# A re-ordered front end in a two-block transformer kernel: index logits between the gate sums, modulation blocks beside two later stages, the reload of x moved

## The reference, cut to what matters

```python
ada = c @ w_ada + b_ada                       # 6 x 1024 numbers: 48 blocks of 128
shift1, scale1, gate1, shift2, scale2, gate2 = split(ada, 6)
h = rms_norm(x, g_norm1) * (1.0 + scale1) + shift1
zq, zk, zv, ziq, zik, ziw, zp, zg = split(h @ w_in)
q, k, ik = rms_norm(zq), rms_norm(zk), rms_norm(zik)
score = sum_h relu(iq_h . ik * idx_scale) * ziw_h          # index logits, 4 heads
sel = top_k(score, 128)                                    # per query, then attention on sel
y_attn = attention(q, k, v, sel) @ w_up_attn
y_pool = pool_mixer(zp, ...) @ w_up_pool                   # windows 2, 4, 8, 16
g_attn, g_pool = split(sigmoid(zg), 2)
x = x + gate1 * ((g_attn * y_attn + g_pool * y_pool) @ w_out)
h2 = rms_norm(x, g_norm2) * (1.0 + scale2) + shift2
x = x + gate2 * peer_ffn(h2, ...)                          # expert query, top 16 of 128 x 128 experts
for i in range(2):                                         # windowed attention, then latent attention
    x = x + mixer_i(rms_norm(x, g_i))
    x = x + (p[i] @ ple_w[i]) * sigmoid(rms_norm(x, ple_g_i) @ ple_w_gate[i])
return rms_norm(x, g_final)
```

## Time and profile before

| | |
|---|---|
| median of 3 runs | 2800.81 us (2798.86 to 2802.94) |
| profiled execution, its own time | 2798.45 us |
| its span | 2796.6 us |
| mean granted TensorE clock | 0.953 of full |
| busy: PE, DVE, POOL, ACT | 2515.2, 1558.5, 1602.1, 594.7 us |
| chain that ended last: PE, DVE, DMA | 77%, 12%, 3% |
| DMA | 375.45 MB, mean 134 GB/s |

### The profile page before, as it was taken

The page is one execution under the profiler, slowest core; times in us unless marked ns, Lnnn a source line. Parts: engine busy times, 40 slices in busy tenths (PEclk is TensorE's granted clock), DMA queues, the critical chain, the costliest instruction groups (busy, mean ns, idle before and its releaser), DMA issues.

```text
span 2796.6 us, 38708 instructions
## 1 busy us (share of the span) xinstructions
PE 2515.2 (90%) x12856; PEld 1260.3 (45%) x12856; DVE 1558.5 (56%) x2823; ACT 594.7 (21%) x1243; POOL 1602.1 (57%) x1048
## 2 busy tenths in 40 slices
PE   3767788999999999978999999999898888989987
PEld 1423443444455555433444444444355533557633
DVE  6498583699967777505952222250218836555525
ACT  1111221111122222201111111110125322245412
POOL 4535435799976767659976666660560157830053
PEclk7878898999999999989999999999999999999998
DMA  6216312354446587577765555560220022310021
GB/s 228 98 44 215 118 38 80 113 150 143 146 147 199 179 249 246 166 217 254 261 220 204 201 204 201 204 224 15 84 83 1 9 75 68 106 53 1 9 75 38
DMA packets 189252, 375.45 MB, mean 134 GB/s; under 512 B 13536, under 2 KB 79200, under 8 KB 189152
## 3 DMA queue, kind: packets, MB, share of 16 engines
q1 hardware_dynamic: 119696, 332.64, 35.8%
q10 hardware_dynamic: 69456, 41.49, 5.0%
HBM read 302.77 MB, written 71.30 MB: 134 GB/s over the span
## 4 chain that ended last, share of the span: by engine, by line
PE 77%; DVE 12%; DMA 3%; issue 2%; ACT 2%; POOL 2%; ACTq 1%; SPq 0%; DVEq 0%; POOLq 0%
PE ps L624 65%; PE ps L714 3%; PE ps L734 3%; PE ps L840 2%; PE ps L723 2%; DMA arena<-ada_w 2%; DVE arena L1280 2%; PE ps L672 1%; ACTq L1097 1%; DVE arena L1384 1%; DVE arena L1383 1%; DVE spare L1190 1%; DVE arena L1245 1%; ACT arena L1016 1%; DVE arena L1218 1%
## 5 line engine op out<-in xcount | busy, mean ns | idle before, releaser
L624 PE MATMUL ps<-hT,parts 128*128 128x512 f16 x4800 | 1070.3, 383 | 66.1 <-DVE hT L1198 29.6
L573 POOL TENSOR_SCALAR parts<-ring 128x1024 f16<-128x1024 f32 x261 | 297.9, 1141 | 955.3 <-PE ps L624 890.0
L624 PEld LDWEIGHTS ps<-hT,parts 128*128 128x128 f16 x4800 | 466.5, 98 | 642.0 <-issue 43.3
L624 PE MATMUL ps<-arena 128*128 128x512 f16 x3072 | 666.2, 380 | 8.4 <-DVE arena L1544 8.4
L576 POOL TENSOR_TENSOR parts<-ring,parts 128x1024 f16<-128x1024 f32 x261 | 577.2, 2212 | 21.7
L624 PEld LDWEIGHTS ps<-arena 128*128 128x128 f16 x3072 | 300.9, 98 | 374.5 <-issue 15.0
L1539 DVE TENSOR_TENSOR arena<-arena 128x512 f32<-128x512 f32 x128 | 149.7, 1170 | 451.6 <-DMA arena<-gate_mem 447.8
L574 POOL TENSOR_SCALAR ring<-ring 128x1024 f32<-128x1024 f32 x261 | 306.6, 1175 | 0.0
L594 POOL TENSOR_TENSOR arena<-ring,arena 128x1024 f16<-128x1024 f32 x128 | 283.6, 2215 | 10.6
L592 POOL TENSOR_SCALAR arena<-ring 128x1024 f16<-128x1024 f32 x128 | 148.2, 1158 | 169.7 <-PE ps L624 169.7
L624 PE MATMUL ps<-arena,parts 128*128 128x512 f16 x876 | 199.8, 389 | 49.4 <-POOL parts L576 34.3
(11 more groups left out here) (169 smaller groups left out, 2414.6 us busy)
## 6 DMA issues: line engine op xcount, KB each, us to landing
ring<-w SPq DMA_DIRECT2D x133, 512.0 KB, 3.3
ring<-u SPq DMA_DIRECT2D x128, 512.0 KB, 3.9
ring<-v SPq DMA_DIRECT2D x128, 512.0 KB, 3.4
act_mem<-spare SPq DMA_DIRECT2D x128, 256.0 KB, 4.0
gate_mem<-arena ACTq DMA_DIRECT2D x4, 8192.0 KB, 42.0
arena<-act_mem SPq DMA_DIRECT2D x128, 256.0 KB, 3.6
arena<-gate_mem SPq DMA_DIRECT2D x128, 256.0 KB, 3.8
arena<-ada_w SPq DMA_DIRECT2D x48, 512.0 KB, 4.8
```

The costliest lines, as they stand in the source:

```text
L573: G.tensor_scalar(dst[:, 0, :], src, WS, 1.0, ALU.mult, ALU.mult).then_inc(scaled, 1)
L624: ins = [T.matmul(out_, a, b, start=start and j == 0, stop=stop and j == 2) for j, (a, b) in enumerate(((lhs[0], rhs[0]), (lhs[0], rhs[1]) ...
```

## The change

1. First norm: all 16 first blocks have slots of their own, SP issues them with no wait, in turn with the first four weight tiles. DVE forms only the 8 scale blocks ahead of the norm; each shift block is formed in the norm's loop, ahead of its product.
2. Index logits: PE turns q and k after two of the four zp sums, and the logits of query blocks 1, 2 and 3 stand ahead of gate sums 0, 5 and 10. ACT's relus and DVE's pool groups 2 and 3 move with them. ACT takes the root of the q and k statistics ahead of iq and zp.
3. The other 32 blocks: 24 are formed three at a time ahead of each of out's 8 residual additions, with `c_row` copied to PSUM, and 8 (gate2) ahead of each peer_q sum. Their 7 slots are dead buffers; SP loads the first 7 once attention has begun, the others behind out's and peer_q's tiles, each when the block of 7 places earlier has been used.
4. up_attn's sum with the gates is made in PSUM banks 6 and 7 instead of `scr`.
5. Norms 1 and 3 to 6: the squares and their matmuls go between the sums of the stage before (`behind`, lag of two sums); norms 4 and 6 square into `aq`. ple_w0 and ple_w1 are read by ACT around the root. A square root of one column (`warm`) stands ahead of each last square.
6. The reload of x stands behind the last gelu instead of ahead of the last 16.

The diff, cut to its core:

```diff
-        ADA_A, ADA_B = 16, 32
+        ZG_SPLIT = (5, 10)
+        ADA_FIRST = [8 + k for k in range(KC)] + [k for k in range(KC)]
+        ADA_LATER = [b + k for k in range(KC) for b in (16, 24, 32)] + [40 + k for k in range(KC)]
+        LATER = 7
...
+            def load_later(n):
+                if n >= LATER:
+                    sp.wait_ge(ada_used, len(ADA_FIRST) + n - LATER + 1)
+                sp.dma_start(ada_later[n % LATER], ada_in[ADA_LATER[n]]).then_inc(ada_loaded[n % LATER], 16)
...
-            zg = stages["zg"].t0
-            weights(RING, zg + 4, RING)
...
-            weights(zg + 16, T_EXP, zg + 16)
+            first_out, first_peer = stages["out"].t0, stages["peer_q"].t0
+            weights(RING, first_out, RING)
+            sp.wait_ge(max_ready, U_SPARSE + 1)
+            for n in range(LATER):
+                load_later(n)
+            for m in range(KC):
+                load(first_out + m, w_in[first_out + m])
+                for n in range(LATER + 3 * m, min(LATER + 3 * m + 3, 3 * KC)):
+                    load_later(n)
+            for m in range(KC):
+                load(first_peer + m, w_in[first_peer + m])
+                load_later(3 * KC + m)
...
-            features("zg", hr)
+            index_logits(1)
+            features("zg", hr, last=ZG_SPLIT[0])
+            index_logits(2)
+            features("zg", hr, first=ZG_SPLIT[0], last=ZG_SPLIT[1])
+            index_logits(3)
+            features("zg", hr, first=ZG_SPLIT[1])
...
-            features("out", in_parts(gT), lambda k: pe.wait_ge(tok_ready, 3 + k + 1))
-            norm(1)
+            features("out", in_parts(gT), lambda k: pe.wait_ge(tok_ready, 3 + k + 1), behind(1, 2))
+            last_parts(1, 2)
...
-            features("ple_w0", in_parts(pT), lambda k: pe.wait_ge(p_ready, k + 1))
-            norm(3)
-            features("ple_g0", hr, h_need(3))
-            norm(4)
+            features("ple_w0", in_parts(pT), lambda k: pe.wait_ge(p_ready, k + 1),
+                     lambda m: norm_part(3, KC - 3 + m) if m in (1, 2) else None)
+            features("ple_g0", hr, h_need(3), behind(4, 2))
+            last_parts(4, 2)
...
-            act.dma_start(xT[:, :, :], x_park.rearrange("c p n -> p c n")).then_inc(x_back, 16)
             gelus(AT_GATES + S // GROUP, CHUNKS)
+            act.dma_start(xT[:, :, :], x_park.rearrange("c p n -> p c n")).then_inc(x_back, 16)
...
-            for m in range(ADA_A):
-                modulate(m)
+            for n in range(KC):
+                first_block(n)
             own.settle()
             gains(0, 8, "g_norm1")
-            norm(0, lambda k: gain[:, 0, k:k + 1], lambda k: ada[:, k:k + 1])
+            norm(0, lambda k: gain[:, 0, k:k + 1], lambda k: ada[:, k:k + 1], shift_block)
...
-            for m in range(ADA_A, ADA_A + ADA_B):
-                modulate(m)
...
-                dst = scr[:, m % 2, :]
+                dst = ps[:, 6 + m % 2, :]
...
+            c_psum = ps[:, 4:6, :].rearrange("p a b -> p (a b)")
+            own.link(V.tensor_copy(c_psum, c_row))
+            def gate_blocks(m):
+                for n in range(3 * m, 3 * m + 3):
+                    later_block(n, c_psum)
+                own.settle()
+                own.link(V.tensor_scalar(gate1[:, m:m + 1], ada[:, 16 + m:17 + m], 1.0 / WS, None, ALU.mult))
+            residual("out", lambda m: gate1[:, m:m + 1], gate_blocks)
```

More of the change, by code:

```diff
@@ L630, in piece, with features @@
                 return w[:, 0, a:a + width], w[:, 1, a:a + width]
-            def features(name, rhs, need=None):
+            def features(name, rhs, need=None, after=None, first=0, last=None):
                 st = stages[name]
-                for m in range(st.outs):
+                for m in range(first, st.outs if last is None else last):
                     need_bank(st.s0 + m)
@@ L642, in features @@
                             need(k)
-                        first, last = three(bank(st.s0 + m), piece(n, (at % PER) * P, P), rhs(k), k == 0,
+                        head, tail = three(bank(st.s0 + m), piece(n, (at % PER) * P, P), rhs(k), k == 0,
                                             k == st.kc - 1)
                         if at % PER == 0:
-                            first.then_inc(begun, 1)
-                    last.then_inc(summed, 1)
+                            head.then_inc(begun, 1)
+                    tail.then_inc(summed, 1)
+                    if after is not None:
+                        after(m)
             def tokens(name, lhs, need=None):
@@ L980, in copy, with square, norm @@
                 return A.activation(dst, src, ACT.Copy, scale=scale)
-            def norm(n, need, shift_of=None):
-                for k in range(KC):
-                    need(k)
-                    own.do(A.activation(hT[:, k, :], xT[:, k, :], ACT.Square), squares)
+            def square(n, k, need):
+                if k == KC - 1:
+                    own.do(A.activation(warm[:, n:n + 1], eps[:, 0:1], ACT.Sqrt))
+                need(k)
+                own.do(A.activation(squares_of(n)[:, k, :], xT[:, k, :], ACT.Square), squares)
+            def norm(n, need=None, shift_of=None, between=None):
+                if need is not None:
+                    for k in range(KC):
+                        square(n, k, need)
+                if between is not None:
+                    between(-2)
                 act.wait_ge(norm_sum, n + 1)
@@ L989, in norm @@
                     return
+                if between is not None:
+                    between(-1)
                 for k in range(KC):
+                    if between is not None:
+                        between(k)
                     act.wait_ge(norm_whole, KC * n + k + 1)
@@ L1124, in _, with embedded @@
             attention(units_window(), U_WINDOW)
-            take("ple_w0", lambda s, b: copy(ple[:, s, :], b))
             def ple_gate(name, n):
-                norm(n, x_from("a_out" if n == 3 else "b_out"))
+                def embedded(k):
+                    first, last = {-2: (0, 3), -1: (3, 6), 1: (6, 7), 2: (7, 8)}.get(k, (0, 0))
+                    take("ple_w0" if n == 3 else "ple_w1", lambda s, b: copy(ple[:, s, :], b), first, last)
+                norm(n, x_from("a_out" if n == 3 else "b_out"), between=embedded)
                 def gate(s, b):
@@ L1133, in gate, with of_sum @@
                     return A.activation(gate_t[:, s % 2, :], b, ACT.Sigmoid, scale=1.0 / WS)
-                take(name, gate)
+                def of_sum(k):
+                    act.wait_ge(x_ready, (0 if name == "ple_g0" else KC) + k + 1)
+                for s in range(KC + 1):
+                    if s < KC:
+                        take(name, gate, s, s + 1)
+                    if s >= 1:
+                        square(n + 1, s - 1, of_sum)
             ple_gate("ple_g0", 3)
-            norm(4, lambda k: act.wait_ge(x_ready, k + 1))
+            norm(4)
             take("b_c", lambda s, b: copy(lat[:, s, 0:512], b))
@@ L1163, in _ @@
             act.wait_ge(turned_read, 14 + KC + 5 + 2 * B_H + KC)
-            take("ple_w1", lambda s, b: copy(ple[:, s, :], b))
             ple_gate("ple_g1", 5)
-            norm(6, lambda k: act.wait_ge(x_ready, KC + k + 1))
+            norm(6)
             for k in range(0, KC, 2):
@@ L1182, in take, with norm @@
                 return bank(st.s0 + s)
-            def norm(n, g_of, shift_of=None):
+            def norm(n, g_of, shift_of=None, beside=None):
                 dve.wait_ge(norm_root, n + 1)
@@ L1209, in norm @@
                         dve.wait_ge(h_ready, KC * n + k - 1)
+                    if k < KC and beside is not None:
+                        beside(k)
                     if k < KC:
```

142 lines of the change are left out of this document (83 added, 59 removed).

## The result

The changed kernel takes 2720.15 us (median of four runs, 2717.65 to 2725.41), the kernel before 2799.89 beside it (2798.86 to 2802.94): a ratio of 0.9716, 95% interval 0.9699 to 0.9733. The profiled execution took 2717.65 us, its span is 2715.8 against 2796.6, and the mean granted clock 0.968 against 0.953. I had forecast 2711 us, in a range of 2680 to 2745.

The account below looks back on a forecast made before the run. PE's own work was taken to bound the kernel where PE is full, so only its idle time could be won. Terms -4 - 5 - 69.6 - 8.5 + 33.7 + 1 - 20.6 - 14 gave -87: 2711 us, range 2680 to 2745.

Parts of the forecast that it names:

- what to look for: Signs expected in the profile; for out, four waits of PE of about 10 us released by POOL's cut.
- step 3: Logits, selection and gates to up_pool: PE's queue slightly longer than DVE's, -69.6 us, bounds -75 and -55.
- step 5: out: weight tiles wait behind modulation loads on SP, 22 us for two sums instead of 10.4; +33.7 us.
- The rival that DVE is the bound in the front: Held rounds in the first norm (+10), held pool groups and scores (-57): +26, 2737 us; chance 8%.
- term 1: First norm: eight rounds of 5.3 us, q ends near 72 us instead of 76.3; -4 us, bounds -19 and +19.
- rival A: out's tiles are early after all, PE never waits: out costs -5 instead of +33.7, 2673 us; chance 10%.
- step 2: Up to the first index logit: half of PE's 10.32 us wait for the normalised rows goes, -5 us.
- Step 7: Reload of x: PE's 22.56 us wait goes, 2 us lost meeting the expert stage's second-half loads; -20.6 us.
- Step 8: Norms 3 to 6: waits behind them shrink, norm 3 -7.5, norm 4 about +0.5, twice each; -14 us.
- The slower rival: out's loop closes for each sum, not for two: +147 where the forecast has +34, 2824 us; chance 2%.

Follow-up runs that it names:

- both repairs: The changed kernel with out's weight tiles loaded three ahead and the pool groups' last sum and result in PSUM: 2668.50 us, ratio 0.9531; again 2668.89 us.

## Why the prediction was right, and where it was not

The time fell inside the range, 9 us above the number. Of the mechanisms that I had named, one is not in the trace: PE is not busy without a gap from the first index logit to up_pool, since DVE is the longer queue there. The others are: the pool tile in time, three waits of PE in out released by POOL's cut (what to look for said four; the sum's own rounds had three), SP's tile loads right behind the third block, the blocks at 1.28 us, no long issue on ACT, ple_g0 1.58 us behind ple_w0. That the sum came out near is in part luck: step 3 gave 14.4 us less than its number and step 5 cost 4.1 more, while steps 1, 2 and 7 gave 10.9 more. The terms:

*Step 3 failed in its bound: -55.2 for -69.6,* the very edge of its bounds. I had PE's queue as the longer, 90.1 us against DVE's 86; DVE's is. DVE took 106.0 us from the first index logit to the end of the last selection: 7.5 before the first score (pool groups 0 and 1 were not done, held beside POOL: a sum of 0.68 us took 2.54), 21.3 for the first selection where I took 18.4 from the earlier trace rows, 21.2 for pool groups 2 and 3 where I took 14, 25.0 for the second where I took 23.2, 30.9 for the third as I took it. In DVE's timeline of the changed kernel:

```profile
116.63 2.54 DVE L1430 TENSOR_TENSOR arena<-arena 128x511 f32<-128x511 f32 x1
...
119.28 0.68 DVE L1430 TENSOR_TENSOR arena<-arena 128x510 f32<-128x510 f32 x1
...
125.63 0.35 DVE L1456 TENSOR_SCALAR arena<-arena 128x256 f32<-128x256 f32 x1
126.10 4.59 DVE L1458 SCALAR_TENSOR_TENSOR arena<-arena 128x256 f32<-128x256 f32 x3
```

The first selection's 18.4 us came from a stretch in which POOL stood still (0.00 busy in 134 to 176 us), and I had added time beside POOL to the pool groups only, and too little: beside POOL three scores took 4.59 us where the kernel before has 1.67. So PE waited 9.47 + 2.44 us, and after the wait up_pool ran below full clock for a part, 2.3 us more for 96 matmuls than at the earlier trace rows's speed. The rival that DVE is the bound in the front had this term right (-57 to -55.2) and the first one wrong: term 1 gained, it did not lose 10. The runs with PSUM sums and with shortened sums showed DVE's length to be the bound; with both repairs the third selection ends at 208.2 instead of 224.1, and the bound changes to PE.

By the locking rule of the Trainium skill (SBUF — State Buffer, "Who interferes with whom") I had 7 us for a round of the first norm. The rounds were 4.8 us in the mean, (62.73 + 1.62 - 25.75) / 8, from DVE's rows:

```profile
25.75 1.78 DVE L1347 CUSTOM_DVE_ANT_0 arena<-arena,route,vecs 128x1024 f32<-128x1024 f32 x1
...
30.98 2.48 DVE L1256 SCALAR_TENSOR_TENSOR spare<-xT,gain,spare 128x512 f32<-128x512 f32 x1
...
50.25 3.03 DVE L1347 CUSTOM_DVE_ANT_0 arena<-arena,route,vecs 128x1024 f32<-128x1024 f32 x1
...
53.33 0.75 DVE L1256 SCALAR_TENSOR_TENSOR spare<-xT,gain,spare 128x512 f32<-128x512 f32 x1
...
62.73 1.62 DVE L1266 SCALAR_TENSOR_TENSOR hT<-spare,ada,hT 128x512 f16<-128x512 f32 x2
```

Instructions are held, a block up to 3.03 us for 1.28 and a product 2.48 for 0.75, which agrees with that section of the Trainium skill, and an operand in PSUM lifts it (1276 against 1863 ns, the cleanest pair of this study); but not each of three instructions waits for a whole one of POOL. A rule that says whether two instructions meet does not say how often.

*Step 5, the loss that I had put at +33.7, was +37.8.* Counted from the end of up_attn, sums 1, 3 and 5 end at 22.9, 45.1 and 68.4 us for 22.5, 44.4 and 66.3: the round is 22.7 us for 22. Behind sum 5 nothing waits, so the norm parts between sums 5, 6 and 7 are paid, two of 0.86, where I had all six in waits; the last part adds 0.3. That is the 4.1. The run with three tiles ahead is rival A made on purpose: 2682 us where I had 2673, the same 9 by which the forecast was low.

*Steps 1 and 2, -16.2 for -9,* had the sign right and the reason by half. I had the rounds begin at 28 us and take 5.3 each, with q's end near 72; they began at 25.75 and took 4.8, and q ended 4.6 us behind the last one, at 69.0. Against the kernel before, only 3.6 of the 7.3 us come from the blocks' place in DVE's order. The other 3.8 come from the place of their loads, which I had not read: before, DVE waited 5.12 us for block 8, and my rounds silently had none of that wait. Of step 2's 8.9 us, 5.8 are the shorter wait for the normalised rows (4.49 for 10.32, about half as I took it), and 3.3 a second wait of PE, between the turns and the first logit, which two zp sums now fill. I had not read it:

```profile
134.32 1.22 PE L771 MATMUL ps<-arena 64*128 64x256 f32 x4 [3.30 <-DVE arena L1342]
```

*Step 7, -24.3 for -20.6:* the 2 us for the reload's meeting the second half's loads did not come. PE's waits at the start of that half are 2.49 and 4.40 us, no longer than the 2.51 and 5.88 before.

*Step 8, -13.3 for -14,* term by term: norm 3 -6.3, norm 5 -8.0, norms 4 and 6 +0.3 and +0.65. By the Trainium skill (ScalarE: Activation LUTs, "What ACT_TABLE_LOAD costs") the last two would have been 1.2 us dearer each. The trace does not agree: ACT's row is 1.28 us for the load, its next activation begins 0.02 us after the load's end (2276.03), and PE waited 0.91 us there for the last square.

The slower rival (a loop that closes for each sum) is out: SP issues tiles at 344.24 and 348.81, 367.43 and 372.60, two for each round.

What stays open: why the two repairs gave some 7.5 us more together. By the traces 5.9 of it lie in the front (up_pool ends at 236.1, not 242.0), though the two kernels issue the same loads up to there; 1.7 lie in out, whose rounds took 85.0 us in the trace with the pool sums alone against 83.3 in the changed kernel, which is within what out varies by. In the front DVE's third selection ends 8.9 us earlier than with the pool sums alone (208.2 for 217.1), and no single place holds this: 2.3 us come before the first score, 1.9 in the first selection, 2.0 in pool groups 2 and 3, 0.9 in the second selection and 1.8 in the third. It is no accident of one execution: the trace of the same kernel run again has the end of up_pool at 236.8. Which DVE instruction is held goes with where POOL's cuts fall beside it; what moved them the traces do not show. The times of this kernel also spread wider than the others (2664 to 2677 us).

## What to carry to other kernels

When loads with waits are put between the weight tiles of a queue, the distance from the last gating instruction to the tile's use is issue, landing and cut, here 10 us for each round. Read that list first, and put several tiles ahead of the gated loads. Durations read from a stretch in which another engine rests are lower bounds once work is moved beside it. Price what is moved as held, and give one operand or the result a place in PSUM where banks are idle. Count every DMA of a moved step, also for what it was waiting on before. When two queues are nearly as long as each other, take both as the bound: here the one that I had put 4 us behind was the longer by some 10 (106.0 us against PE's 95.5 from the first logit to the end of the gate sums, waits included).

## What the runs showed of the hardware

An issue of a DMA on ACT's queue directly behind the issue of an 8 MB store took 30.47 us and held ACT's own work for all of it; the same issue 82 us after the store's took 0.38, in the changed kernel. The store's own issue took 0.38.

One instruction of 1276 ns on DVE rose to 1863 in the mean beside POOL's cuts with both inputs in SBUF, and not at all with one of them in PSUM. POOL's cut of a tile rose from 4.3 to 7.0 us beside the first kind and not beside the second.

After a wait of 14.80 us PE's next 48 matmuls took 13.09 us, where 10.5 is full speed; after 8.75 us 24 took 6.82 where 5.3 is. The granted clock was 0.50 in the last 8.6 us of the wait ahead of 354.65, 0.63 in the first 7 us behind it and 1.00 after. So the three waits in out each cost their own length and 1.5 to 2.6 us behind it. In the trace of the reload put back, sums behind such waits took up to 8.23 us, 2.9 more than at full clock.

A load of ACT's activation table took 1.28 us, and the next activation began 0.02 us behind it.
